# Expert sums back to back: where VectorE splits the activations between two halves of a slot, and which product of a half slot gives its signal

## What is computed

```python
a = jnp.einsum('cd,ced->ce', x_c, u[e_c])                   # each token against its chosen experts
w = jax.nn.gelu(a.astype(jnp.float32), approximate=False).astype(x_c.dtype) * g_c
return jnp.einsum('ce,ced->cd', w, v[e_c])                  # weighted sum of the experts' output rows
# further layers:
h = jax.nn.silu(u @ w_ffn_gate[l]) * (u @ w_ffn_up[l])
x = x + gt_f * (h @ w_ffn_down[l])
```

## Time and profile before

| | |
|---|---|
| median of 3 runs | 2092.24 us (2090.78 to 2092.31) |
| profiled execution | 2090.81 us, of which 2089.0 us span |
| mean granted TensorE clock | 0.995 |
| PE matmul busy | 2018.9 us (97%), 13416 instructions |
| PE weight loads busy | 1811.4 us (87%) |
| VectorE, ScalarE busy | 1526.3 us (73%), 1102.9 us (53%) |
| chain that ended last | PE 80%, VectorE 7%, issue 6% |
| back-to-back expert sums | 484.70 to 626.22 us |

### The profile page before, as it was taken

One profiled execution on the slowest core, in us unless ns is written; L12 is line 12 of the kernel. 1 busy time (PEld: TensorE's weight loads), 2 busy tenths in 40 slices (PEclk: granted clock), 3 DMA queues, 4 the chain that ended last, 5 costly groups with the idle time before them and its releaser, 6 DMA issues.

```text
span 2089.0 us, 41368 instructions
## 1 busy us (share of the span) xinstructions
PE 2018.9 (97%) x13416; PEld 1811.4 (87%) x13416; DVE 1526.3 (73%) x3580; ACT 1102.9 (53%) x2262; POOL 209.3 (10%) x218
## 2 busy tenths in 40 slices
PE   8999999879999999999999999999999999999998
PEld 7769988767779999999989898899998978899997
DVE  5766797797668888888876377877775647777775
ACT  3243655795444444444456465654455555655444
POOL 0000499681000000000000000000000000000000
PEclk9999999999999999999999999999999999999999
DMA  8335545203558877878745533445553553355552
GB/s 305 122 131 166 188 162 164 86 0 123 179 194 303 290 278 288 285 281 288 267 139 173 189 120 107 152 163 187 184 184 129 173 171 112 105 162 180 188 183 100
DMA packets 103532, 375.94 MB, mean 180 GB/s; under 512 B 11504, under 2 KB 11776, under 8 KB 103168
## 3 DMA queue, kind: packets, MB, share of 16 engines
q1 hardware_dynamic: 89280, 323.86, 46.3%
q10 hardware_dynamic: 14144, 50.72, 6.4%
HBM read 373.47 MB, written 1.05 MB: 179 GB/s over the span
## 4 chain that ended last, share of the span: by engine, by line
PE 80%; DVE 7%; issue 6%; POOL 3%; ACT 2%; DVEq 1%; ACTq 0%; DMA 0%; POOLq 0%
PE bank L773 14%; PE bank L779 14%; PE bank L776 14%; PE bank L823 8%; PE bank L826 7%; PE bank L829 7%; POOL part_lo L1636 3%; PE bank L575 3%; PE bank L730 1%; DVE one_hots L1928 1%; PE bank L1031 1%; PE bank L987 1%; PE bank L1069 1%; DVE part_lo L2075 1%; PE bank L946 1%
## 5 line engine op out<-in xcount | busy, mean ns | idle before, releaser
L1259 ACT ACTIVATE part_hi<-ring 128x512 fp32r<-128x512 f32 x1108 | 682.3, 627 | 413.0 <-PE bank L776 242.3
L1763 DVE TENSOR_TENSOR part_lo<-ring,part_hi 128x512 fp32r<-128x512 f32 x712 | 473.1, 689 | 210.4 <-ACT part_hi L1259 200.4
L773 PE MATMUL bank<-u_hi,part_hi 128*128 128x256 f32 (+1 forms) x1904 | 546.6, 287 | 14.5 <-POOL part_lo L1636 10.2
L779 PE MATMUL bank<-u_hi,part_lo 128*128 128x256 f32 (+1 forms) x1904 | 534.1, 281 | 0.0
L776 PE MATMUL bank<-u_lo,part_hi 128*128 128x256 f32 (+1 forms) x1904 | 532.9, 280 | 0.0
L773 PEld LDWEIGHTS bank<-u_hi,part_hi 128*128 128x128 f32 (+1 forms) x1904 | 356.3, 187 | 27.4 <-POOL part_lo L1636 12.2
L776 PEld LDWEIGHTS bank<-u_lo,part_hi 128*128 128x128 f32 (+1 forms) x1904 | 356.6, 187 | 4.5
L779 PEld LDWEIGHTS bank<-u_hi,part_lo 128*128 128x128 f32 (+1 forms) x1904 | 358.6, 188 | 0.5
L2075 DVE TENSOR_TENSOR part_lo<-ring,part_hi 128x512 fp32r<-128x512 f32 (+1 forms) x312 | 211.1, 682 | 109.8 <-ACT part_hi L1259 104.3
L823 PE MATMUL bank<-part_hi,w_hi 128*128 128x512 f32 x688 | 274.6, 399 | 4.3 <-DVE w_lo L1966 2.2
L826 PE MATMUL bank<-part_hi,w_lo 128*128 128x512 f32 x688 | 268.4, 390 | 0.0
(11 more groups left out here) (287 smaller groups left out, 2928.6 us busy)
## 6 DMA issues: line engine op xcount, KB each, us to landing
ring<-stream_dram SPq DMA_DIRECT2D x606, 512.0 KB, 3.3
arena<-ada_dram ACTq DMA_DIRECT2D x96, 512.0 KB, 4.5
xT<-x_dram SPq DMA_DIRECT2D x4, 256.0 KB, 5.8
arena<-mem_dram SPq DMA_DIRECT2D x1, 1024.0 KB, 9.7
arena<-keys_dram SPq DMA_DIRECT2D x1, 1024.0 KB, 7.2
out_dram<-uT SPq DMA_DIRECT2D x4, 256.0 KB, 2.5
cst<-consts_dram SPq DMA_DIRECT2D x1, 841.0 KB, 14.2
cond<-cond_dram SPq DMA_DIRECT2D x1, 512.0 KB, 15.0
```

The lines of the kernel that those rows point to most:

```text
L773: m = pe.matmul(o, hi, u(cc), start=first, stop=False, **flags)
L779: m = pe.matmul(o, lo, u(cc), start=False, stop=last, **flags)
L1259: act.activation(part_hi[:, h % 4, 0:width], ring[:, n % RING, (h % 2) * width:(h % 2 + 1) * width], ACT.Copy).then_inc(hi_ready, 1)
L1763: v.tensor_tensor(part_lo[:, h % 4, :], ring[:, n % RING, (h % 2) * 512:(h % 2 + 1) * 512], part_hi[:, h % 4, :], ALU.subtract).then_inc(l ...
```

## The change

In `sum_half` the first product of every half now gives `half_begun`, and the second product of an even half gives `slot_begun`. In `sum_ahead` VectorE splits the activations of slot k between the low part of the slot's first half and that of its second, where before it split them after both. Nothing is added or removed: the same instructions run on every engine.

```diff
@@ sum_half (L821 to L829)
                     m = pe.matmul(o, w_hi[:, wi, rows], hi, start=first, stop=False, skip_group_check=True)
+                    if tt == 0:
+                        m.then_inc(half_begun, 1)
+                    m = pe.matmul(o, w_lo[:, wi, rows], hi, start=False, stop=False, skip_group_check=True)
                     if tt == 0 and h % 2 == 0:
                         m.then_inc(slot_begun, 1)
-                    m = pe.matmul(o, w_lo[:, wi, rows], hi, start=False, stop=False, skip_group_check=True)
-                    if tt == 0:
-                        m.then_inc(half_begun, 1)
                     m = pe.matmul(o, w_hi[:, wi, rows], lo, start=False, stop=False, skip_group_check=True)
@@ VectorE
+            def low_half(h, turns):
+                rest_of_half(S_PEER + h // 2, h, turns * 24 + PQ_HALVES)
+
@@ sum_ahead (L1993)
                 for k in range(12):
-                    if k or not isinstance(it, int):
-                        low_parts(AHEAD + k, it)
+                    late = k or not isinstance(it, int)
+                    if late:
+                        low_half(2 * (AHEAD + k), it)
                     weigh_ahead(k, it)
+                    if late:
+                        low_half(2 * (AHEAD + k) + 1, it)
```

## The result

The changed kernel takes 2080.0 us (median of 5 runs, 2078.0 to 2082.9), the kernel before beside it 2092.3 us (5 runs, 2090.8 to 2093.1); the ratio is 0.9943, with a 95% interval of 0.9929 to 0.9956. The profiled execution took 2081.1 us, its span 2079.3 us, 9.7 us less than before.

A forecast was written before the change was run, and what follows sets the result against it. TensorE was taken as the bound, stalled once per back-to-back slot by late activations. 9.0 us there plus 0.5 us at the feed-forward ends: 2092.24 - 9.5 = 2082.7 us (2081.3 against the profiled execution); range 2079.8 to 2087.5.

The forecast's parts named there:

- The place and the circle: Back-to-back sums: signals through TensorE, ScalarE and VectorE set the 2.95 us slot; 47 boundaries lose their stall, 9.0 us.
- The new order's slack: Back-to-back stage: `w_lo` gets 1.4 us of slack; VectorE reaches the second low part 1.11 us after the slot's start.
- The parts not additive: Back-to-back stage: the earlier `half_begun` would nearly suffice by itself; with VectorE's new order it only adds slack.
- just about enough: Back-to-back stage: the earlier `half_begun` in VectorE's old order takes 0.24 us off a circle of 2.95, barely sufficient.
- The end of the feed-forward parts: Ends of both feed-forward parts: `half_begun` one product earlier shortens TensorE's last wait by 0.23 us each, 0.5 us together.
- the pace between stalls: Back-to-back stage, an unknown size: 0.230 us a product taken, 2.76 us a slot, from ten steps in the stage.
- the other end: Later stage's 0.227 us a product: 2.72 us a slot, which would save 10.8 us and give 2080.9.
- The clock: Half-clock stretches, seen between feed-forward part and next layer, move with the shift: 1 us or so either way.
- TensorE's own queue: Rival: the gap between back-to-back slots is TensorE's queue; only 11 written-out slots gain, 2.6 us, 2089.6; chance 0.07.
- Denser and slower: Rival: busier VectorE and ScalarE slow back-to-back products to 0.24 us, 2088.4, or 0.235, 2085.5; chance 0.11 for the pair.
- The ring: Rival: later `slot_begun` delays load refills, 8.0 us slower, 2100.3; decides only beyond 5.9 us of cover; chance 0.03.
- 216 ns a product: Skill's rule for 512-column matmuls: a 2.59 us slot in the back-to-back stage, saving 17 us, time 2074.8.

The follow-up runs named there:

- signals alone: Kernel before with only the two signals of `sum_half` exchanged, VectorE's order unchanged: 2081.8 us, ratio 0.9957.
- old order with the late signal: Kernel before, with `half_begun` given by the fourth product of a half instead of the second: 2113.9 us against 2091.0, ratio 1.011.
- new order with the doubled delay: Changed kernel's VectorE order, `half_begun` on the fourth product, ScalarE waiting one more half in the back-to-back stage: 2115.6 us against 2091.2, ratio 1.0116.
- order alone: Kernel before with only VectorE's order in `sum_ahead` changed, signals of `sum_half` as before: 2081.3 us against 2091.0, ratio 0.9951.
- new order with the late signal: Changed kernel's VectorE order, `half_begun` on the fourth product of a half, `slot_begun` on the first: 2081.8 us, ratio 0.9956.
- the one of the fifth of pace: Changed kernel with SyncE's refills two slots later, first try: profiled execution 10336.7 us with TensorE at a fifth of its pace, the other 2083.3 us.
- 14.7 us in 17 places: Changed kernel with SyncE's refills two slots later from the expert slots on, second try: 2080.7 us, ratio 0.9949.
- refilled one slot later still: Changed kernel with SyncE's refills three slots later from the expert slots on: 2239.6 us in a single execution.

## Why the prediction came out right, and where it was off

**The place and the circle: right.** The stall lay in the back-to-back stage and the circle TensorE, ScalarE, VectorE set the slot; with delayed signals, in the old order and in the new, the slot came out at the sum of the circle's legs to 0.02 us.

**The new order's slack: right.** Forecast 1.4 us for `w_lo` and 1.11 us to the second low part; in the trace 1.38 and 1.09.

**The parts not additive: right**, down to the signals alone being "just about enough".

**The end of the feed-forward parts: right.** 0.23 us each, as forecast.

**The term that was mis-sized: the pace between stalls.** I took 0.230 us a product, measured over ten steps in the stage itself, 2.76 us a slot. Without stalls the slot is 2.72 us, 0.227 a product, and 47 x (2.951 - 2.72) = 10.9 us are saved in place of 9.0. The pace of the later stage, which I named as the other end, was the right one; my row was nearer in place but not in kind, because the stall was still in it. In the kernels with a late weight load (before, old order with the late signal, new order with the doubled delay) the steps behind the first product take 0.230 us on average, 0.231 to 0.234 for the first two and 0.227 for the last two; in the three without (changed, order alone, new order with the late signal) 0.227 throughout; with the signals alone, where the load is only 0.12 us late, 0.228. So the slower pace follows the late load and fades within the slot, in either order of VectorE's work. Why a late load slows the ten products after it, no run settles.

**The clock: a term I left as 1 us either way.** The changed kernel's stage came out 9.24 us shorter, not 10.9. Its trace has the granted clock at 0.50 from 485.0 to 488.4 us, at the lower level of 1.2 GHz; products there are 0.43 us apart, and the first slot takes 4.44 us. Where the drop is missing (order alone, and one of the other two traces of the same changed kernel) the first slot takes 2.85 or 2.86 us. The stage is 132.28 us with the drop and 130.7 without: 1.6 us. Ahead of it lies the building of the grid, where TensorE waits for the one-hots between short groups of products. The code there is the same in both kernels. So two errors cancelled in the profiled execution: +1.9 us of pace, -1.6 of clock. That it took 2081.1 us where 2081.3 were forecast, and that the stage was 132.3 us long where 132.5 were, is luck to that extent. The drop was in five of the twelve traces of the kernels other than before, the one of the fifth of pace left out, and in two of the changed kernel's three; the third has a stretch of the same length at 394.2 us instead, ahead of the stage. The one trace of before has neither, so whether the change makes it likelier is open. The later half-clock stretches moved too, by 0.7 us one way and 1.1 the other, which is the "1 us or so either way" of the prediction.

**The time.** Over all runs here the means are 2091.2 us before (31 runs, standard deviation 1.3) and 2080.5 after (15 runs): 10.7 us less. 10.8 of the stage and 0.5 of the ends, less a clock drop of 1.6 us in some executions, come near that; the first two medians are 12.3 us apart because single runs spread over some us. The forecast of 2082.7 was 9.5 us less than before.

**The rivals.** *TensorE's own queue*: the label "issue" in the earlier trace rows was the wait for `w_lo`, seen through a register. It went away in the loop as in the slots written out, and with the late signal it grew, now put down to VectorE's instructions. *Denser and slower*: the opposite; the denser stage runs faster products. *The ring*: real, but more than 5 us away.

The Trainium skill's 216 ns a product ("TensorE: Matmul & The Clock Gate", "Back-to-back issue gap") is not reached without stalls either: 227 ns. The prediction left out that the same section calls this figure the isolated gap and gives about 131 ns for a sustained stream of weight loads and products, which is what this stage is. No run here comes near that figure; it is further from the 227 ns than the one used.

## What to carry to other kernels

When an engine idles a little in every turn of a loop, follow the signals round until the legs add up to the period; if they do, moving any one of them by a product's time, or moving what isn't needed yet behind what is, gives the stall back until the next bound, and a second such edit gives nothing. Delay the same signal on purpose: the circle must grow by exactly that, and in the new form it must not, as long as the delay is within the slack. And take the unstalled pace from a stage that has no stall, not from the steps between stalls.

## What the runs showed of the chip that I had not expected

- After a weight load that comes late, the next products of 128x512 run at 0.230 us on average instead of 0.227, easing off within ten products.
- A stretch of 3.4 us at half clock can fall into the start of the stage behind the grid, in some executions of one kernel and not in others; it costs 1.6 us. That can account for part of the 6 us over which runs of the changed kernel spread (2076.9 to 2082.9).
- Loads that make ScalarE wait 14.7 us in 17 places cost TensorE only 1.6 us, at the two longest; refilled one slot later still, the loads cost 150 us.
